# An output-gate tile and the last input chunk among the mLSTM pieces of two token mixers

## The reference, cut to what matters

```
qkv_a, a_a, b_a, z_a, qkv_b, qk_c, v_c, i_c, f_c, o_c = split(h @ w_in)
oa = gated_delta_rule(...)                       # 6 heads, chunk by chunk
oa = oa * rsqrt(mean(oa * oa) + eps) * gdn_norm * silu(z_a)
ob = moba_attention(qb, kb, vb)                  # 4 heads
hc = mlstm(qc, kc, v_c, i_c, log_sigmoid(f_c))   # 6 heads:
     # P = qk * exp(D - m);  h = (P @ v) / max(|sum P|, exp(-m))
hc = norm(hc * sigmoid(o_c)) * mlstm_norm
y  = concat(oa, ob, hc) @ w_out
```

## Time and profile before

| what | us |
|---|---|
| median of 3 runs | 1969.62 (1967.79 to 1970.97) |
| profiled execution | 1969.99 |
| its span | 1968.10 |
| mean granted TensorE clock | 0.976 |

### The profile page before, as it was taken

The page is one execution under the profiler, slowest core; times in us unless marked ns, Lnnn a source line. Parts: engine busy times, 40 slices in busy tenths (PEclk is TensorE's granted clock), DMA queues, the critical chain, the costliest instruction groups (busy, mean ns, idle before and its releaser), DMA issues.

```text
span 1968.1 us, 30880 instructions
## 1 busy us (share of the span) xinstructions
PE 1869.1 (95%) x13104; PEld 1606.2 (82%) x13104; DVE 1260.6 (64%) x2244; ACT 707.6 (36%) x941; POOL 130.3 (7%) x68
## 2 busy tenths in 40 slices
PE   7999999998999989998999989998999998889997
PEld 4999888877999989998888789998744555646896
DVE  3877665534888677675673469998794677325712
ACT  3333243223633263334332263332521344224322
POOL 0000063300000000003440000000000000000000
PEclk9999999989999999999999899999999999999999
DMA  9777623422577637663334046676153010222100
GB/s 386 294 277 258 236 97 132 180 86 107 208 263 286 237 149 268 238 245 141 135 145 194 22 150 236 266 269 232 76 188 146 1 43 1 88 107 86 65 22 22
DMA packets 47257, 323.83 MB, mean 165 GB/s; under 512 B 4960, under 2 KB 8160, under 8 KB 8336
## 3 DMA queue, kind: packets, MB, share of 16 engines
q1 hardware_dynamic: 47120, 321.85, 43.0%
HBM read 320.78 MB, written 1.05 MB: 164 GB/s over the span
## 4 chain that ended last, share of the span: by engine, by line
PE 85%; DVE 9%; ACT 3%; issue 1%; SPq 1%; DMA 1%; DVEq 0%; ACTq 0%
PE ps L346 83%; DVE wk L1825 3%; ACT wk L1327 2%; DVE wk L1822 2%; DVE wk L1819 2%; PE ps L349 1%; SPq L1302 1%; DVE low L1819 1%; ACT L1327 1%; DMA ring<-in_stream_dram 1%; DVE xa L1822 0%; DVE xlo L1819 0%; DVE tab L1819 0%; DVE small L2297 0%; ACT xa L1327 0%
## 5 line engine op out<-in xcount | busy, mean ns | idle before, releaser
L346 PE MATMUL ps<-xa,ring 128*128 128x256 f32 (+1 forms) x1648 | 429.0, 419 | 17.5 <-ACT xa L1327 11.6
L346 PEld LDWEIGHTS ps<-xa,ring 128*128 128x128 f32 x1648 | 314.5, 193 | 117.4 <-issue 72.2
L346 PE MATMUL ps<-xhi,low 128*128 128x256 f32 x1408 | 388.8, 284 | 0.0
L346 PE MATMUL ps<-xhi,whi_wk 128*128 128x256 f32 x1088 | 306.9, 293 | 19.1 <-ACT xhi L1327 12.4
L1327 ACT ACTIVATE wk<-ps 128x256 f32<-128x256 f32 (+4 forms) x221 | 109.6, 503 | 574.3 <-PE ps L346 499.7
L346 PE MATMUL ps<-xlo,whi_wk 128*128 128x256 f32 x1088 | 297.6, 282 | 0.0
L346 PEld LDWEIGHTS ps<-xhi,low 128*128 128x128 f32 x1408 | 263.7, 191 | 0.0
L1327 ACT ACTIVATE whi_wk<-ring 128x2048 fp32r<-128x2048 f32 x100 | 191.0, 1914 | 197.1 <-DMA ring<-in_stream_dram 110.2
L1825 DVE SCALAR_TENSOR_TENSOR wk<-ring,sc,wk 128x256 f32<-128x256 f32 x576 | 233.9, 477 | 0.0
L346 PE MATMUL ps<-wk 64*64 64x64 f32 (+10 forms) x2712 | 223.2, 271 | 10.6 <-ACT wk L1327 8.5
L1819 DVE TENSOR_TENSOR low<-ring,whi_wk 128x2048 fp32r<-128x2048 f32 x100 | 228.1, 2284 | 0.3 <-ACT whi_wk L1327 0.3
(11 more groups left out here) (116 smaller groups left out, 2536.6 us busy)
## 6 DMA issues: line engine op xcount, KB each, us to landing
ring<-in_stream_dram SPq DMA_DIRECT2D x302, 1024.0 KB, 5.9
tab<-in_tab_dram SPq DMA_DIRECT2D x1, 1376.0 KB, 22.5
res<-in_xt_dram SPq DMA_DIRECT2D x1, 1024.0 KB, 21.0
res<-in_ct_dram SPq DMA_DIRECT2D x1, 1024.0 KB, 8.6
out_dram<-wk SPq DMA_DIRECT2D x2, 512.0 KB, 3.0
tab<-in_tab_dram SPq DMA_DIRECT2D x1, 256.0 KB, 2.9
cols<-in_cols_dram SPq DMA_DIRECT2D x1, 242.5 KB, 2.8
tab<-in_wg_dram SPq DMA_DIRECT2D x1, 96.0 KB, 5.4
```

Of the source, the lines that this page charges most:

```text
L346: last[0] = nc.tensor.matmul(o, l, r, start=start, stop=stop, skip_group_check=free)
```

## The change

The list of pieces gets a new order; no piece is added, taken away or altered, and no other line changes.

```diff
-             "mt3", "p5.0", "mo1", "p5.1", "p11.0", "p11.1"]
-          + ["lm0", "lm1", "lm2", "lb0", "lb1", "ls0", "ls1", "lb2", "lx0", "lb3", "ls2", "lb4", "lb5", "ls3", "ls4", "q15", "lx1", "ls5", "lx2"])
+             "mt3", "p5.0", "mo1", "p5.1"]
+          + ["p11.0", "lm0", "lm1", "lm2", "p11.1", "lb0", "lb1", "ls0", "q15", "ls1", "lb2", "lb3", "lx0", "ls2", "lb4", "ls3", "lb5", "ls4",
+             "lx1", "ls5", "lx2"])
```

## The result

| | before | after |
|---|---|---|
| median, 6 runs each | 1970.3 us | 1977.85 us |
| lowest to highest | 1967.79 to 1974.28 | 1973.32 to 1983.02 |
| profiled execution | 1969.99 | 1976.63 |
| its span | 1968.1 | 1974.8 |

The changed kernel is slower: the ratio of the times is 1.0036, 95% interval 1.0022 to 1.0049. The forecast was 1980, in a range of 1973 to 1987.

A forecast was written before the change was run, and what follows sets the result against it. PE was taken as the bound, busy 95% of the span. Per mixer front -1.9, tail +4.95 and clock at early +2.2 gave +5.25, two mixers +10.5: 1980 us, in a range of 1973 to 1987.

The forecast's parts named there:

- the two mechanisms: Behind oa: DVE's strict order lengthens the way to early, +4.95 us per mixer; early starts at half clock, +2.2.
- the tail: From the end of oa to early: grows from 12.55 to 17.5 us per mixer, +4.95 (+4.3 at full clock).
- a sign against itself: At the start of early: the prediction is wrong if PE keeps full clock into it; 0.50 was expected.
- the first front at 31 us at most: From the start of p11.0 to the end of oa: 28.7 to 31 us, less than 13.65 at half clock.
- Front: From p11.0 to the end of oa: 1.9 us shorter per mixer, with bounds of -3.1 and +5.4.
- DVE order: Behind oa: DVE must finish lx0 before oa_e, which starts 5.9 us after oa instead of 3.07.
- ls5 behind the reader of ls4: Before early: ls5 waits for DVE's reading of ls4, so early starts 16.9 to 17.5 us after oa.
- Clock at early: At early: PE starts at half clock after idle stretches and loses 1.5 to 2.8 us per mixer, taken as 2.2.
- ACT's extra table loads: In the front on ACT: two more sigmoid/exp switches per mixer, 1.28 us each, taken as hidden and charged 0.
- front clock holds wholly: Rival: front at full clock, -3.1 us, tail as forecast; +4.05 per mixer, 1977.7 us; chance 0.18.
- front at half clock as before: Rival: p11.1 or q15 also run slow, front +3 to +5.4 us per mixer, 1990 to 1994 us; chance 0.07.
- no loss of clock in the tail: Rival: early starts at full clock 16.9 us after oa; total 1972 or 1970.5 us, not slower; chance 0.10.

The follow-up runs named there:

- experiment 9: The changed kernel plus ten unused products in PE's waits (two behind ls2, two behind lb4, six behind lx1): 1977.66 us, 1.0031 of the kernel before.
- experiment 5: The changed kernel with ls5 issued by PE behind early(1, 0) instead of in front of it: 1976.84 us, 1.0029 of the kernel before.
- experiment 2: The kernel before with only p11.1 moved behind lm2: 1965.31 us, 0.9968; run a second time, 1963.8 us, 0.9971.
- experiment 1: The changed kernel with lx0 put back in front of oa, lb2 and lb3 behind it: 1974.73 us, 1.0017 of the kernel before.
- experiment 8: The changed kernel with lx0 back in front of oa, plus eight unused products per mixer behind lx1: 1970.93 us, 1.0000 of the kernel before.
- experiment 7: The kernel before with p11.1 behind lm2, ls3 in front of lb5, and ls5 behind early(1, 0): 1966.61 us, 0.9981 of the kernel before.

## Why the prediction came out as it did

The direction, the two mechanisms and the size held; 1980 was 2.2 us too high, since the change per mixer was +3.6 and +4.2 and not +5.25. Some of the agreement is luck, for the errors cancel in part: on average the front gave 1.0 us less back than forecast, the tail cost 0.9 less and the clock at `early` 1.4 less.

The prediction named as a sign against itself that PE keeps full clock into `early`. In the profiled execution that happened in the first mixer and not in the second. It had also put the first front at 31 us at most; it was 31.73. What carries the result is the tail: 16.26 us at full clock throughout (experiment 9) is 3.7 per mixer, nearly all of the difference.

- *Front, forecast -1.9 (bounds -3.1 to +5.4).* Measured -0.1 and -1.7. Too hopeful in the first mixer: `q15` ran at half clock and took 6.58 instead of 3.84. The dense piece did bring the clock back, as said, but paid for it itself.
- *DVE order, `oa_e` at 5.9 after `oa`.* Measured 5.70 in both mixers, and 16.26 to `early` with the clock at 1.00 (experiment 9), where the full-clock figure was 16.9. The forecast end of `oa_done` was 15.4, measured 14.9: I had put small gaps between DVE operations that in the trace overlap slightly, so that ACT's exps ended 8.5 after `oa` and not 9.0. That `lb4` on PE must wait for DVE's reading of `lx0` (its place is two further on, in the same bank) I had missed; it cost nothing, because DVE was not free for it sooner.
- *ls5 behind the reader of ls4.* Forecast 1.5 to 2.1 from `oa_done` to `early`, measured 1.36 and 2.10. Right. What I did not see is that removing that wait gives nothing (experiment 5).
- *Clock at early, forecast 2.2 us lost per mixer.* This is the mis-sized term: 0 in the first mixer, 1.5 in the second. In the first the fall came earlier, at 440.8; it stretched the last pieces of the tail inside PE's waits, and the clock was back at 447.6, before `early` began. The forecast had the fall certain and the return only behind `early`.
- *ACT's extra table loads, charged 0.* Right. The load that leads to the exp of `lm0` and the exp itself stand like this in the changed kernel:

```profile
405.15 0.38 ACT L1328 ACTIVATE res<-ps 128x256 f32<-128x256 f32 x1 [1.91 <-PE ps L347]
405.55 1.28 ACT L1328 ACT_TABLE_LOAD   x1
406.84 0.38 ACT L1328 ACTIVATE wk<-ps 128x256 f32<-128x256 f32 x1
```

The exp starts 1.29 us after the load does. The Trainium skill ("ScalarE: Activation LUTs", What ACT_TABLE_LOAD costs) adds a drain of about 1.38 us per switch; these rows have no room for it, and experiment 2, with all the extra switches, is faster than the kernel before.

The rivals: *front clock holds wholly*, -3.1, did not come (-1.7 and 3.4 us of half clock in the second mixer is the forecast's own -1.9); *front at half clock as before* did not come; *no loss of clock in the tail* came in the first mixer of the profiled execution only, by its outcome (6.82 us ran at half clock, at no cost in time), and even there the DVE order kept the sum at +3.6.

What the parts of the change are worth, from the runs: `p11.1` between `lm2` and `lb0` gains 0.3%, measured on two chips, of which the parts hold less than half. `q15` out of the wait loses: the same kernel without and with that move (experiments 2 and 1, which differ further in the order of the `lb` and `ls`) goes from 0.9968 to 1.0017. The late `lx0` adds the rest, from 1.0017 to 1.0036; these two intervals overlap a little, and the tails of 14.1 and 13.9 against 16.25 and 16.98 carry that reading. They do not add up as single edits: `lx0` late costs 0.72% alone, and 0.19% on top of the others, and a likely reason is that `q15` and `p11.1` then stand in front: the fronts of the changed kernel have 6.83 and 3.42 us of half clock where `lx0` late alone has 27.31 and more, running on into the tail. No run with `lx0` late has just one of the two in front to show it. What exactly decides in which execution a dense piece meets the fall stays open.

## What to carry to other kernels

A long unbroken run of TensorE products inside a wait can be worth more than its length: where it stood, the clock of what followed stayed up in some kernels here (experiments 2 and 8) and not in another (9). So before moving it out, look at the granted clock of the stretch behind the wait. In a list that several engines walk strictly in order, follow each moved piece on every engine: here the PE side of `lx0` was short, and its five DVE operations landed on the chain. And if PE is the bound behind a wait, expect nothing from an earlier start that is bought by moving PE work behind it: in experiments 5 and 7 it gave no gain that could be told.

## What was not expected of the hardware

Adding eight unused products (3.72 us of TensorE work per mixer) did not lengthen a kernel and probably shortened it, from 1.0017 to 1.0000 of the time before. And taking one piece, `lx0`, from in front of `oa` left the clock at 1.2 GHz for 27 us and more in both mixers (416.4 to 443.7 in the first) where it had been 13.65, which made a shorter front 2.8 us longer.
